# Differential attention: logits, their maxima and the negation in one VectorE pass

## The reference

```python
def diff_attention(q, k, v, lam, rel_bias):
    ...
        s = jnp.einsum('bhcqd,bhckd->bhcqk', q_blk, kt).astype(jnp.float32) * dh ** -0.5
        s = jnp.where(dist >= 0, s + bias[None, :, None], -jnp.inf)
        p = jax.nn.softmax(s, axis=-1)
        attn = p[:, :, 0] - lam * p[:, :, 1]
        return jnp.einsum('bhqk,bhkv->bhqv', attn.astype(v.dtype), vt)
```

## Time and profile before

| | |
|---|---|
| median of three runs | 3002.89 us |
| lowest and highest | 2996.98 and 3004.61 us |
| the profiled execution, its own time | 3005.15 us |
| its span, first to last instruction | 3003.4 us |
| mean granted TensorE clock | 0.950 of full speed |
| TensorE, VectorE, ScalarE, GpSimd busy | 91%, 54%, 35%, 16% of the span |
| the edited stage, from the first logits to the first split of the next layer | 2430.67 to 2522.48 us |

### The profile page before, as it was taken

The page is one execution under the profiler, slowest core; times in us unless marked ns, Lnnn a source line. Parts: engine busy times, 40 slices in busy tenths (PEclk is TensorE's granted clock), DMA queues, the critical chain, the costliest instruction groups (busy, mean ns, idle before and its releaser), DMA issues. The chain is left out here.

```text
span 3003.4 us, 33355 instructions
## 1 busy us (share of the span) xinstructions
PE 2738.1 (91%) x13110; PEld 2185.5 (73%) x13110; DVE 1616.5 (54%) x2261; ACT 1039.9 (35%) x1582; POOL 495.2 (16%) x383
## 2 busy tenths in 40 slices
PE   6898999799899999969988997999997977799996
PEld 4676999577678888747777985787785855587775
DVE  3745664454456653454435754677634365567744
ACT  4653321533343222334234343222223345322222
POOL 4544443001010000000001433100022021400002
PEclk9999899899999999989988998999999988899998
DMA  4423000432023223212210001122322210122231
GB/s 142 141 92 134 1 1 1 165 105 92 22 91 105 99 86 97 77 64 77 92 56 1 2 1 56 63 92 91 106 92 81 99 36 24 47 91 91 90 106 50
DMA packets 82628, 222.10 MB, mean 74 GB/s; under 512 B 13293, under 2 KB 29950, under 8 KB 81284
## 3 DMA queue, kind: packets, MB, share of 16 engines
q1 hardware_dynamic: 76960, 204.96, 21.1%
q10 hardware_dynamic: 5512, 15.01, 1.4%
HBM read 213.60 MB, written 11.58 MB: 75 GB/s over the span
## 5 line engine op out<-in xcount | busy, mean ns | idle before, releaser
L230 DVE TENSOR_TENSOR w_low<-w_raw,w_high 128x1024 fp32r<-128x1024 f32 (+2 forms) x338 | 410.0, 1215 | 889.0 <-ACT w_high L220 888.9
L292 PE MATMUL bank<-x_high,w_high 128*128 128x512 f32 x1840 | 747.5, 406 | 63.6 <-DVE x_low L482 37.5
L293 PE MATMUL bank<-x_low,w_high 128*128 128x512 f32 x1840 | 735.1, 400 | 0.0
L294 PE MATMUL bank<-x_high,w_low 128*128 128x512 f32 x1840 | 732.1, 398 | 0.0
L220 ACT ACTIVATE w_high<-w_raw 128x1024 fp32r<-128x1024 f32 (+2 forms) x380 | 386.2, 1019 | 625.7 <-PE bank L294 503.2
L292 PEld LDWEIGHTS bank<-x_high,w_high 128*128 128x128 f32 x1840 | 349.8, 190 | 181.7 <-issue 63.7
L293 PEld LDWEIGHTS bank<-x_low,w_high 128*128 128x128 f32 x1840 | 349.8, 190 | 87.6 <-issue 6.1
L294 PEld LDWEIGHTS bank<-x_high,w_low 128*128 128x128 f32 x1840 | 349.4, 190 | 84.1
L292 PE MATMUL bank<-f_high,w_high 128*128 128x512 f32 x528 | 208.9, 396 | 0.9 <-DVE w_low L230 0.9
L294 PE MATMUL bank<-f_high,w_low 128*128 128x512 f32 x528 | 209.0, 396 | 0.0
L293 PE MATMUL bank<-f_low,w_high 128*128 128x512 f32 x528 | 209.0, 396 | 0.0
(11 more groups left out here) (595 smaller groups left out, 4382.4 us busy)
## 6 DMA issues: line engine op xcount, KB each, us to landing
w_raw<-in_ffn_in_dram SPq DMA_DIRECT2D x132, 512.0 KB, 3.4
w_raw<-in_ffn_out_dram SPq DMA_DIRECT2D x48, 512.0 KB, 3.5
w_raw<-in_gdn_in_dram SPq DMA_DIRECT2D x24, 512.0 KB, 3.4
w_raw<-in_mix_in_dram SPq DMA_DIRECT2D x22, 512.0 KB, 3.7
w_raw<-in_ffn_out_dram SPq DMA_DIRECT2D x24, 384.0 KB, 3.2
w_raw<-in_swa_qk_dram SPq DMA_DIRECT2D x12, 512.0 KB, 3.5
bias_rows<-bias_row ACTq DMA_DIRECT2D x4, 1280.0 KB, 15.0
w_raw<-in_mix_gate_a_dram SPq DMA_DIRECT2D x8, 512.0 KB, 3.4
```

The lines of the kernel that those rows point to most:

```text
L230: (on or self.nc.vector).tensor_tensor(self.low[c % SPLIT][:, 0:w], self.raw[c % RAW][:, 0:w], self.high[c % SPLIT][:, 0:w].bitcast(F32), ...
L292: nc.tensor.matmul(out, wh, high[:, k, :], start=first + at == 0, stop=False)
L293: nc.tensor.matmul(out, wh, low[:, k, :], start=False, stop=False)
L294: last = nc.tensor.matmul(out, wl, high[:, k, :], start=False, stop=first + at == depth - 1)
```

## The change

Instead of multiply-and-add, maximum and negation, VectorE runs one `tensor_tensor_reduce` for each component. It writes -(scores + bias) and keeps the least of these values, which is the negated maximum. ScalarE's exponential turns the sign back with scale -1. The factor 1/8, for which the fused instruction has no place, moves to ScalarE's copy of the query blocks, in the region ahead. The semaphore `max` goes: the exponentials wait for `logits`.

```diff
@@ odd_mixer_region, ScalarE
-                act.wait_ge(R["max"], t + 1)
+                act.wait_ge(R["logits"], t + 1)
                 for i in range(2):
                     a = L[t % 2][:, i * w:(i + 1) * w]
-                    ins = nc.scalar.activation(a, a, ACT.Exp, bias=nmax[:, t % 2, i:i + 1], accum_out=tot[:, t % 2, i:i + 1])
+                    ins = nc.scalar.activation(a, a, ACT.Exp, scale=-1.0, bias=nmax[:, t % 2, i:i + 1], accum_out=tot[:, t % 2, i:i + 1])
@@ odd_mixer_region, VectorE
                 bias = TZ[:, hd, 384 - c * P:384 - c * P + w]
-                steps(nc.vector.scalar_tensor_tensor(L[p][:, 0:w], PS[2 * p][:, 0:w], 64 ** -0.5, bias, ALU.mult, ALU.add))
-                nc.vector.scalar_tensor_tensor(L[p][:, w:2 * w], PS[2 * p + 1][:, 0:w], 64 ** -0.5, bias, ALU.mult,
-                                               ALU.add).then_inc(R["logits"], 1)
-                steps.wait()
-                steps(nc.vector.reduce_max(nmax[:, p, 0:1], L[p][:, 0:w], AX_X))
-                dve.wait_ge(R["logits"], t + 1)
-                steps(nc.vector.reduce_max(nmax[:, p, 1:2], L[p][:, w:2 * w], AX_X))
-                steps.wait()
-                nc.vector.tensor_scalar(nmax[:, p, :], nmax[:, p, :], -1.0, None, ALU.mult).then_inc(R["max"], 1)
+                for i in range(2):
+                    last = nc.vector.tensor_tensor_reduce(L[p][:, i * w:(i + 1) * w], PS[2 * p + i][:, 0:w], bias, -1.0, 3e38,
+                                                          ALU.add, ALU.min, nmax[:, p, i:i + 1])
+                last.then_inc(R["logits"], 1)
@@ layer_region, ScalarE
-                W.freed(nc.scalar.activation(odd["qk"][:, n, :], W.bank(PS, "diff_qk", n)[:], ACT.Copy), "diff_qk", n)
+                if n < 4:
+                    W.freed(nc.scalar.activation(odd["qk"][:, n, :], W.bank(PS, "diff_qk", n)[:], ACT.Copy,
+                                                 scale=64 ** -0.5), "diff_qk", n)
+                else:
+                    W.freed(nc.scalar.activation(odd["qk"][:, n, :], W.bank(PS, "diff_qk", n)[:], ACT.Copy), "diff_qk", n)
```

More of the change, by code:

```diff
@@ L2662, in tile_of @@
         return t // NT, t % NT, (t % NT + 1) * P
-    with region(nc, "scores", "logits", "max", "exp", "probs", "turned", "turned_sb", "pv", "out", "own", "a_sums", "k_turned",
+    with region(nc, "scores", "logits", "exp", "probs", "turned", "turned_sb", "pv", "out", "own", "a_sums", "k_turned",
                 "o_sums", "s_sums", "d_sums", "g_sums", "rows_turned", "rows_ok", "am", "a_turned", "ker", "o", "o_sq", "d_sq", "g_read", "d_read", "log", "rstd", "at", "st",
```

## The result

The changed kernel takes 2981.2 us (median of four, 2977.09 to 2990.43) against 3003.38 us before: ratio 0.9935, interval 0.9905 to 0.9964. Measured twice more on other occasions, with more executions, it comes to 0.9954 (0.9938 to 0.9971) and 0.9949 (0.9933 to 0.9965), that is 12.3 and 13.8 us between medians.

A forecast was written before the change was run, and what follows sets the result against it. TensorE is busy 91% overall, but the edited stage's bound changes by step; savings where TensorE or ScalarE waits for VectorE sum to 1.85 + 2.7 + 3.1 + 1.6 = 9.25 us, so 3002.89 - 9.2 = 2993.7 us, range 2988.0 to 3001.0.

The forecast's parts named there:

- The delivery: Differential-attention stage, VectorE: handing over each fused pass's least value takes 0.08 us a pass, with zero and 0.24 as ends.
- Half rate: Rival: the fused pass streams at half rate like the scan, two passes about 2.3 us at 512 columns; 2998.5 us, chance 0.16.
- a load: Rival: VectorE pays 1.28 us per fused pass to load the function, as ScalarE does for tables; 3021.8 us, chance 0.04.
- the loop of logits, weighing and turn: Stage steps: VectorE makes logits of t, weighs t-1, TensorE turns t-1, then VectorE writes logits of t+1; 9.25 us saved.
- plus 3 us for medians that themselves spread from 2996.98 to 3004.61: Whole kernel: allowance for varying medians, added to the likeliest case's 2991 to 2996 us.
- at t = 4 VectorE already waits for L2710 ..., nothing: Head 1, first step: VectorE already waits for the gated-linear-attention matmuls (about 0.75 us), so the change gives nothing.
- at t = 12 it waits again: Head 3, first step: VectorE waits again for the gated-linear-attention matmuls, so the change gives nothing.
- a moving clock: Sign of a wrong forecast: the clock of the edited stage moves; no size given.
- GpSimd: Stage: VectorE stands beside GpSimd products; 0.55 us returned at t = 5 and 9, 0.7 charged at 7 and 11, 0.4 at 2.
- The scale: Query-block copies on ScalarE: moving the factor 1/8 there costs nothing (584 against 580 ns); exposed, 0.02 us.
- more comes through: Rival: TensorE keeps 2.4 GHz at t = 4 and 12 and lost GpSimd overlap is nothing; 12.6 us, 2990.3 us, chance 0.13.
- TensorE as the bound: Rival: TensorE bounds the middle heads, or GpSimd's standing worsens; 3 to 5 us lost, about 2998 us, chance 0.17.

## Why the prediction was wrong, point by point

**The fused pass.** Right at the lower bound: 0.61 us at 512 columns. The delivery, for which 0.08 us a pass was added, costs nothing on the path although the profile shows it as an instruction. The rule that was cited from the Trainium skill ("VectorE: DVE Perf Modes", section "Two Vector instructions with no wait between them"), that such an operation is two instructions, is borne out by the row; the price put on it was mine, and wrong. The 0.15 us of waiting in its upper end came from no row, and none of it appeared. The "1.28 without delivery" was a slip: twice 0.61 is 1.22, as measured. So VectorE's block got shorter by 1.37, 0.98, 0.83 and 0.56 us, for 1.25, 1.0, 0.7 and 0.4. Half rate (1.2 us) and a load (1.28 us) did not happen.

**The path.** Right in kind: the loop of logits, weighing and turn, with TensorE ending last at t = 0, 1 and 13, which gave 0, 0 and 0.15 us. The sizes, step by step, in the two profiles (13.44 us in all):

```
t           2     3     4     5     6     7     8     9    10    11    12    14    15 and tail
predicted  0.60  1.25  0     1.25  0.90  0.55  0.40  1.25  0.90  0.55  0     0.50  1.10
measured   1.13  1.32  1.25  1.53  0.63  0.98  0.41  1.52  0.64  1.25  1.13  0.58  0.95
```

**The steps that failed** are two, one outside the sum and one in it. What put the time out of the range is "plus 3 us for medians that themselves spread from 2996.98 to 3004.61". The median lies 12.5 us below the forecast, and that is mostly not the mechanism: four executions between 2977.09 and 2990.43 us, compared with a kernel that on its first occasion stood at 3003 and on the next at 2997. The three times shown of it, within 8 us, were too few for the 3 us that were allowed; 29 of it spread over 16. An estimate from the line of equal clocks: from 0.950, the clock of the profiled execution before, to 0.956, the mean of the changed kernel's four, it gives 10 us, and with the 10.7 of the change that is nearly the 22 us between the first medians. (The clocks of the other executions before on that occasion are not on record.)

In the sum, the step that failed is "at t = 4 VectorE already waits for L2710 ..., nothing" and "at t = 12 it waits again": together 2.4 us in these profiles. The reasoning took TensorE's clock of one execution for a property of the kernel; the prediction named a moving clock as a sign of being wrong, and a rival had it, but the sum gave it no term. At the low clock t = 4 still takes 5.8 to 5.9 us in the kernels with the short passes, so there the term of nothing is right within 0.2; at the full clock it takes 4.70. No profile of a kernel with VectorE's passes near their old time had the full clock at t = 4 (0 of 5); of the seven with the short passes four had it. Of the eight profiles in which t = 1 was slow, the five with the old passes were slow at t = 4 as well, and the three with the short ones were not. That more of them get it would be a second gain of the change; it was seen, in few profiles, but its cause was not settled, and filling TensorE's waits did not bring it about. At t = 12 three kernels with the old passes took 3.33 us, without the fall, and the changed one takes 2.81: 0.5, not 1.13 and not nothing.

**GpSimd** was charged too much: 0.7 us at t = 7 and 11, where at most 0.1 was measured. At t = 5 and 9 the standing had been put at 0.55, and taking the products away gave 1.2 and 1.5. In these four steps the sum was too low by 1.4 us; at t = 6 and 10 it was too high by 0.5 together. At t = 2 the 0.4 charged did not come in this profile, and the step gave 0.5 more than was put down: the weighing's two passes took 1.24 us there for 1.44 before. Where t = 1 ran at the full clock, t = 2 took 4.04 us for 3.72, and the charge was due.

With t = 4 at nothing, t = 12 at 0.5, t = 11 as t = 7 (that step too had part of its length from the clock), the measured steps sum to 11.3 us; equal clocks over whole executions give 10.7, the medians of the larger measurements 12.3 and 13.8. The forecast of 9.2 was low by 1.5 to 2 us by the first two, and by 3 to 4.6 by the medians. Taken from 3002.89 us, 10.7 to 11.3 would have been 2991.6 to 2992.2, inside the range: the account of the path was right in the main, and the base it was taken from was not one to rely on.

**The scale** in ScalarE's copies cost nothing that shows (0.58 us a copy with it and without). **Rivals:** "more comes through" named the right place (t = 4 and 12 at 2.4 GHz) and gave 2990.3 us; the measured median lies beyond it for the reason given above; that fewer gaps are what keeps the clock is not shown. TensorE as the bound does set t = 5 and 9 now (busy 2.78 of 2.92 us), but at a length below the old one.

## What to carry to other kernels

Read the gain of a shorter pass from the engine that waits for it, step by step: the same edit gave 1.3 us a step where TensorE waited and 0.1 us in eleven where it was busy 4.35 of 4.35 us. A short operation that GpSimd holds up can cost more than its own standing, for everything behind it on the engine waits too: a negation that stood 0.55 us cost 1.24. Before a step is compared between two profiles, look at its granted clock, and before 10 us in 3000 are compared, take many executions, or the span of the edited stage alone: here one kernel spread over 16 us, almost all of it ahead of the stage.

## What the runs showed of the hardware that was not expected

The read of VectorE's accumulator (0.08 us) lies wholly under the start of the next pass. A fused pass that takes its first value from SBUF and not from the instruction lasts longer: 0.35 us at 128 columns (window stage) against 0.29. There it also waits for the pass before it, and two such passes start 0.40 us apart, where two of the other kind start 0.21 apart; which of the two causes costs how much was not separated. A pass with both of its fp32 sources in SBUF, the weighing's last, took 0.75 us at 512 columns, so no half rate there either. The granted clock of a step of 3 to 6 us is 0.53 in one execution and 1.00 in the next of the same kernel (t = 1: 6.15 and 2.93 us); in five profiles of kernels with the changed stage as it stands or fused in the window too, one of t = 1 and t = 4 was slow each time, and never both.
